# Row scaling moved behind a product, a shift carried as two extra columns, and part of the modulation rows summed by VectorE

## The chip, the core and the metric

The kernel runs on one core of a Trainium2 chip: TensorE (PE) for matrix products, VectorE (DVE), ScalarE (ACT), GpSimd (POOL), and SyncE (SP), which issues DMAs from memory. Each engine runs its own instructions in order and waits for others on semaphores. The metric is the device time of one execution in microseconds. Lower is better.

## The reference

Two transformer-like blocks run one after the other on 256 tokens of width 2048, in float32. What is computed:

```
# block 1
h = rms_norm(x, norm_gain);  proj = h @ w_in          # 2048 -> 8192: conv h,b,c,z and attention q,k,v,z
y_conv = rms_norm(b * conv(c * h_conv)) * silu(z_conv)
y_attn = rms_norm(causal_attention(norm(q), norm(k), v)) * silu(z_attn)   # 8 heads of 128
x = x + concat(y_conv, y_attn) @ w_out
# block 2, modulated by m = silu(c) @ w_ada + b_ada (6 blocks of 2048: sh_a sc_a g_a sh_m sc_m g_m)
h  = rms_norm(x, norm_attn_w) * (1 + sc_a) + sh_a
hc = rms_norm(ctx, norm_attn_w) * (1 + csc_a) + csh_a  # the same two blocks for c_ctx
q, k, v, u = split(h @ w_in_2);  kc, vc from hc @ w_in_2
x = x + g_a * (concat(window_attention, pool(u)) @ w_out_2)
hm = rms_norm(x, norm_mlp_w) * (1 + sc_m) + sh_m
x = x + g_m * (square(relu(hm @ w_up)) @ w_down)       # 2048 -> 8192 -> 2048
out = rms_norm(x, final_norm_w)
```

Only the blocks sh_a and sc_a are needed for c_ctx as well as for c. The other four are needed for c alone.

## The kernel before

**Tiles.** Activations lie transposed: feature on the 128 partitions, 256 tokens on the free axis (`T`), one tile for each of 16 groups of features (`KT`). Every product is written in units. A unit makes one 128x256 output tile from a 128x2048 strip of weights, which comes from memory as two halves of 512 KB into `raw`, a ring of four halves. ACT copies a half to `hi` (fp32r, L731), DVE makes `lo = raw - hi` (L1050), and PE adds up three products for each of the 16 tiles k: hi*x_hi, lo*x_hi, hi*x_lo (`half_unit`, L388; lines 400, 401 and 402). The activations `x` are kept as a pair too, 256 columns of high part and 256 of low part. The down product of the MLP does two of the three in one matmul of 512 columns (`pair_unit`, lines 426 and 427).

**Order.** Everything is written out by hand, and each engine has its own list. ACT and DVE call `split` in unit n for the halves that unit n+2 will use, as soon as PE has released the ring's slot (`w_used`). A unit's result leaves its bank by `evacuate` on ACT (L744) or by an addition on DVE, which counts `evac_done`; PE may start unit n+2 only then.

**Stages.** Units 0 to 31 are eight heads of four units (q, k, v, z): `head_body` on each engine; the scores, probabilities and values of a head are computed during the units of the next one. Units 32 to 63 are eight convolution tiles (`conv_body`). Units 64 to 79 are w_out of block 1 (`out_lap` on DVE, `out_body` on ACT, with the modulation of the context beside it, into `actC`). Then come 8 units of keys and values (80 to 87), 16 of queries and pooling, 16 of w_out_2 (`out_body` and the lap "dve w_out_2"), and four groups of 16 up and 16 down units. ACT and DVE run laps of a loop in most stages; in loops every address that depends on the lap costs register instructions on the engine.

**Modulation.** m needs 96 rows of `w_ada` of 1 MB each (6 blocks of 16 rows). PE takes one row in the middle of each of units 0 to 79, and the last block's during the following units: `ada_rows` (L432), four matmuls of 512 columns into the bank `ADA`, one for each column group, in plain float32 (two passes each). After 16 rows, ACT copies the bank (`ada_copy`, L752), PE turns it (`ada_turn`, L445), and DVE adds the bias (`ada_add`, L1120). The next block's first row waits for `ada_added`. SP loads the rows into two slots of `ada_raw`.

**The norm ahead of the MLP.** In each unit of w_out_2, DVE adds the result to `resid` (L1447), ACT squares it (L903), and DVE adds the square to `sqsum`. After the last one, PE sums over the partitions (`total_sums`), DVE, POOL and DVE make 1/rms on a diagonal, PE broadcasts it over the partitions into `BC`, and then DVE and ACT make the 16 tiles of `actA` four at a time (`norm_tiles`, L1094: times gain and `BC`, plus shift, high part, low part). Up unit 0 waits for each tile (`inA`).

```
def norm_tiles(first, n, gain, shift, src=resid):
    for k in range(first, first + n):
        ins = dve.scalar_tensor_tensor(t4[:, k % 4], src[:, k], gain(k), BC, ALU.mult, ALU.mult)
...
    for k in range(first, first + n):
        low(actA[:, k, 0:T], actA[:, k, T:2 * T], t4[:, k % 4], inA)
```

## Time and profile before

| | us |
|---|---|
| median of 3 runs | 1814.24 (1813.35 to 1815.23) |
| the profiled execution | 1812.95 |
| its span in the trace | 1811.3 |
| PE busy | 1671.5 (92%) |
| DVE busy | 1050.5 (58%) |
| ACT busy | 759.0 (42%) |
| modulation rows on PE (L441), 768 matmul passes | 102.2 busy |

The trace is that of one execution. Matmuls overlap, so "busy" of PE tells little of its pace; the distance from one start to the next does. PE's clock is granted by a throttle and is either full (2.4 GHz) or half (1.2 GHz). The page shows it in tenths over slices of 45 us.

### The profile page before, as it was taken

To read this page: it belongs to the slowest core of one execution; us is meant where nothing else is said; L and a number is where in the kernel's file an instruction comes from. 1 tells how busy PE (TensorE), PEld (TensorE's weight loads), DVE (VectorE), ACT (ScalarE), POOL (GpSimd) and SP (SyncE) were. 2 spreads that over 40 slices of the span, in tenths; PEclk is the share of its full clock that TensorE was granted. 3 is DMA by queue.
4 is the path that set the end of the run, shared out by engine and by line. 5 is a ranking of instruction groups with operands and counts; after the bars stand their busy time and mean duration, and the time that the engine had idled before them with its cause. 6 is when DMAs were issued, how large, how long until landed. Compare 5 with 4: busy or idle time off the path is not lost.

```text
span 1811.3 us, 34903 instructions
## 1 busy us (share of the span) xinstructions
PE 1671.5 (92%) x12462; PEld 1508.9 (83%) x12462; DVE 1050.5 (58%) x1568; ACT 759.0 (42%) x1068; POOL 31.5 (2%) x48
## 2 busy tenths in 40 slices
PE   3899999899988986999889869999999999999996
PEld 2788888788877876878779859989998999899985
DVE  4445454455556557467665575655556555555675
ACT  5344444334333334344344434434443454345442
POOL 0000000000000000000000000000000000000000
PEclk9899999899998998999999969999999999999998
DMA  7677777688874775673225515555555555555552
GB/s 311 242 268 251 276 269 258 214 302 288 301 283 167 286 258 192 256 291 117 94 70 175 176 68 185 185 186 181 180 186 192 183 183 186 185 184 183 185 189 92
DMA packets 88370, 374.71 MB, mean 207 GB/s; under 512 B 10256, under 2 KB 10768, under 8 KB 75488
## 3 DMA queue, kind: packets, MB, share of 16 engines
q1 hardware_dynamic: 87120, 369.54, 59.0%
q0 software_dynamic: 1168, 4.00, 0.7%
q8 instruction: 61, 1.00, 0.2%
q14 instruction: 21, 0.17, 0.0%
HBM read 371.40 MB, written 2.10 MB: 206 GB/s over the span
## 4 chain that ended last, share of the span: by engine, by line
issue 72%; PE 16%; DVE 8%; ACT 3%; POOL 0%; DVEq 0%; ACTq 0%; POOLq 0%
PE G L400 4%; PE G L401 4%; PE G L402 4%; DVE lo L1050 3%; ACT hi L731 1%; PE ADA L441 1%; PE M L624 1%; PE S L611 1%; PE ADA L638 1%; PE S L598 1%; DVE t L1097 0%; DVE resid L1512 0%; DVE sm L1344 0%; DVE blk L1050 0%; PE S L599 0%
## 5 line engine op out<-in xcount | busy, mean ns | idle before, releaser
L1050 DVE TENSOR_TENSOR lo<-raw,hi 128x1024 fp32r<-128x1024 f32 x496 | 607.8, 1225 | 427.9 <-ACT hi L731 396.1
L400 PE MATMUL G<-actA,hi 128*128 128x256 f32 x2368 | 691.8, 292 | 31.7 <-DVE actA L1050 31.1
L731 ACT ACTIVATE hi<-raw 128x1024 fp32r<-128x1024 f32 x496 | 525.6, 1060 | 387.3 <-PE G L427 194.6
L401 PE MATMUL G<-actA,lo 128*128 128x256 f32 x2368 | 676.5, 286 | 0.0
L402 PE MATMUL G<-actA,hi 128*128 128x256 f32 x2368 | 676.2, 286 | 0.0
L400 PEld LDWEIGHTS G<-actA,hi 128*128 128x128 f32 x2368 | 458.6, 194 | 93.0 <-issue 73.9
L401 PEld LDWEIGHTS G<-actA,lo 128*128 128x128 f32 x2368 | 459.2, 194 | 0.4
L402 PEld LDWEIGHTS G<-actA,hi 128*128 128x128 f32 x2368 | 458.7, 194 | 0.0
L426 PE MATMUL G<-actB,hi 128*128 128x512 f32 x1024 | 358.6, 395 | 0.0
L427 PE MATMUL G<-actB,lo 128*128 128x256 f32 x1024 | 287.5, 281 | 0.0
L426 PEld LDWEIGHTS G<-actB,hi 128*128 128x128 f32 x1024 | 192.2, 188 | 44.5
L427 PEld LDWEIGHTS G<-actB,lo 128*128 128x128 f32 x1024 | 194.1, 190 | 0.0
L400 PE MATMUL G<-actB,hi 128*128 128x256 f32 x496 | 144.4, 291 | 1.4 <-DVE lo L1050 0.8
L401 PE MATMUL G<-actB,lo 128*128 128x256 f32 x496 | 141.9, 286 | 0.0
L402 PE MATMUL G<-actB,hi 128*128 128x256 f32 x496 | 141.9, 286 | 0.0
L749 ACT ACTIVATE W<-G 128x256 f32<-128x256 f32 x80 | 30.7, 384 | 201.6 <-PE G L402 201.3
L400 PEld LDWEIGHTS G<-actB,hi 128*128 128x128 f32 x496 | 97.0, 195 | 15.4 <-issue 10.2
L441 PE MATMUL ADA<-ada_raw,cpad 128*32 128x512 f32 x768 | 102.2, 610 | 1.7 <-DMA ada_raw<-w_ada_dram 1.3
L401 PEld LDWEIGHTS G<-actB,lo 128*128 128x128 f32 x496 | 96.9, 195 | 0.1
L402 PEld LDWEIGHTS G<-actB,hi 128*128 128x128 f32 x496 | 96.7, 195 | 0.0
L749 ACT ACTIVATE t<-G 128x256 f32<-128x256 f32 x64 | 24.6, 384 | 118.5 <-PE G L402 118.5
L1050 DVE TENSOR_TENSOR acc<-acc,G 128x256 f32 x96 | 40.4, 421 | 34.3 <-PE G L427 31.7
(173 smaller groups left out, 1004.8 us busy)
## 6 DMA issues: line engine op xcount, KB each, us to landing
raw<-stream_dram SPq DMA_DIRECT2D x496, 512.0 KB, 4.2
ada_raw<-w_ada_dram SPq DMA_DIRECT2D x96, 1024.0 KB, 6.5
x_tok<-x_tok_dram SPq DMA_DIRECT2D x1, 2048.0 KB, 8.3
resid<-xT_dram SPq DMA_DIRECT2D x1, 2048.0 KB, 10.9
ctx_tok<-ctx_tok_dram SPq DMA_DIRECT2D x1, 2048.0 KB, 17.9
W<-ctxT_dram POOLq DMA_DIRECT2D x16, 128.0 KB, 6.1
out_dram<-resid SPq DMA_DIRECT2D x4, 512.0 KB, 2.6
ada_raw<-pool_w_dram POOLq DMA_DIRECT2D x1, 1024.0 KB, 6.9
```

What stands on the lines that cost most here:

```text
L400: pe.matmul(bank, hi[:, slot, cols], x[:, k, 0:T], start=(k == 0), stop=False, skip_group_check=True)
L401: pe.matmul(bank, lo[:, slot, cols], x[:, k, 0:T], start=False, stop=False, skip_group_check=True)
L402: m = pe.matmul(bank, hi[:, slot, cols], x[:, k, T:2 * T], start=False, stop=(k == KT - 1), skip_group_check=True)
L426: pe.matmul(bank[:], hi[:, slot, cols], x[:, k, :], start=(k == 0), stop=False, skip_group_check=True)
L427: m = pe.matmul(bank[:, 0:T], lo[:, slot, cols], x[:, k, 0:T], start=False, stop=(k == KT - 1), skip_group_check=True)
L441: m = pe.matmul(ADA[32 * g:32 * g + 32, :], cpad[:, 4 * (k % 4) + g, 6 - 2 * (k // 4):38 - 2 * (k // 4)], ada_raw[:, n % 2, g, :], start=( ...
L598: pe.matmul(bank[:, 0:T], q, kT[rows, s, :], start=True, stop=False, skip_group_check=True)
L611: m = pe.transpose(S[c][:, k * P:(k + 1) * P], probs[:, c, k * P:(k + 1) * P], ident[:])
L624: m = pe.matmul(M[64 * h:64 * h + 64, 0:T], v[:, k % 2, g:g + 64], turned[:, h, k, :], start=(k == 0), stop=(k == 3), tile_position=(0, 64 ...
L731: return act.activation(dst, src, ACT.Copy)
L749: act.activation(dst, G[j % 2][:, 0:T], func).then_inc(evac_done, 1)
L1050: return dve.tensor_tensor(dst, a, b, op)
```

## The change

There are two parts.

1. **The norm of the MLP.** The up product no longer takes the normed activations but `resid * scale_m`, which does not need 1/rms. It is made tile by tile inside w_out_2: ACT writes the high part with a scale from a pointer (L946 of the changed kernel), DVE the low part (L1525). The 1/rms of each token multiplies the result of a unit instead, on DVE, while the bank is emptied (`scaled`). The shift `sh_m` becomes two more columns of the activations (its high and its low part), so that 2 of the 3 matmuls of each step have 258 columns; the sum of the two result columns is a bias for each output feature, which ACT adds in the Relu. A tile of `actU` is 514 columns long, where one of `actA` is 512. `split` of a unit's second half now stands ahead of the Relu on ACT, and DVE waits for `relu_done`. The up units of group 0 start behind w_out_2 at once; sums and broadcast stand inside the first of them.
2. **Modulation.** Rows 32 to 63 (blocks g_a and sh_m) leave PE. DVE multiplies them by the condition into `part` (`part_take`, 4 instructions of 512 columns for a row, two rows for each head or convolution tile), and after four rows PE sums `part` over the partitions (`part_sums`, 4 matmuls of 1 column); DVE adds the bias (`part_add`). ACT issues the loads of these rows (`part_load`), into slot 1. PE keeps 64 rows: in units 0 to 63 one in every second unit (slot 0, SP), then as before. The loops over heads and convolution tiles on ACT and DVE are written out. Two turns of a block fall away; that at unit 80 moves behind unit 82, and `ada_copy` of block 1 moves ahead of the last tiles of the convolution's norm.

The diff, cut to its core:

```diff
-                unit(at, 1, actA, ada=4 * h + 1)
+                unit(at, 1, actA)
                 if prev:
                     head_turn()
-                unit(at, 2, actA, ada=4 * h + 2)
+                if prev and h % 2 == 0:
+                    part_sums(h // 2 - 1)
+                unit(at, 2, actA, ada=2 * h + 1)
...
+            def part_sums(n):
+
+                pe.wait_ge(ada_taken, 4 * (n + 1))
+                if n:
+                    pe.wait_ge(part_added, n)
+                for m in range(4):
+                    x = pe.matmul(PART[:, m:m + 1], part[:, m * P:(m + 1) * P], ones[:, 0:1], start=(m == 0), stop=(m == 3),
+                                  skip_group_check=True)
+                x.then_inc(part_summed, 1)
...
-            half_unit(at, 0, 0, actC, inC)
-            ada_turn()
-            half_unit(at, 0, 1, actC, inC)
+            unit(at, 0, actC, inC)
             total_sums(1)
...
             unit(at, 2, actC)
+            ada_turn()
             unit(at, 3, actC)
...
-            total_sums(2)
-            broadcast()
...
-                pair_units(8, base, actA, inA if g == 0 else None, 2 * KT)
+                if g == 0:
+                    at = At(base)
+                    pe.wait_ge(shift_ready, 1)
+                    half_unit(at, 0, 0, actU, inA, 2 * KT, extra=2)
+                    total_sums(2)
+                    half_unit(at, 0, 1, actU, inA, 2 * KT, extra=2)
+                    broadcast()
+                    up_unit(at, 1)
+                    up_units(7, base + 2)
+                else:
+                    up_units(8, base)
...
+            def part_load(n, row):
+
+                act.wait_ge(ada_taken, n)
+                src = t_in["w_ada"][row] if isinstance(row, int) else t_in["w_ada"][bass.ds(row, 1)].rearrange("a p n -> (a p) n")
+                act.dma_start(ada_raw[:, 1].rearrange("p k n -> p (k n)"), src).then_inc(ada_full[1], 16)
...
                 split(at, 0, 0)
+                if n:
+                    part_load(2 * n, 2 * KT + 2 * n)
...
                 split(at, 3, 0)
+                part_load(2 * n + 1, 2 * KT + 2 * n + 1)
...
+                    if not ctx_too:
+                        evacuated(at, j)
+                        act.activation(actU[:, u, 0:T], resid[:, u], ACT.Copy, scale=scale_m[:, u]).then_inc(x_hi, 1)
+                        own(x_hi)
                     square(at, j, (sq[:, j % 2:j % 2 + 1], resid[:, u]))
                     split(at, j)
...
+            def part_take(n):
+
+                if n % 4 == 0 and n:
+                    dve.wait_ge(part_summed, n // 4)
+                dve.wait_ge(ada_full[1], 16 * (n + 1))
+                k = n % 4 * 4
+                for m in range(4):
+                    w, c = ada_raw[:, 1, m, :], cpad[:, k + m, 6:7]
+                    if k + m == 0:
+                        seq(dve.tensor_scalar(part[:], w, c, None, ALU.mult))
+                    elif m < 3:
+                        seq(dve.scalar_tensor_tensor(part[:], w, c, part[:], ALU.mult, ALU.add))
+                    else:
+                        dve.scalar_tensor_tensor(part[:], w, c, part[:], ALU.mult, ALU.add).then_inc(ada_taken, 1)
+                        own(ada_taken)
...
                     split(at, j)
+                    dve.wait_ge(x_hi, turn.next("x_hi"))
+                    dve.scalar_tensor_tensor(actU[:, u, T + 2:], resid[:, u], scale_m[:, u], actU[:, u, 0:T], ALU.mult,
+                                             ALU.subtract).then_inc(inA, 1)
+                    own(inA)
                     add_squares(j % 2)
...
-            for b in range(4):
-                norm_tiles(4 * b, 4, lambda k: scale_m[:, k:k + 1], lambda k: adav[:, 0, SH_M + k:SH_M + k + 1])
...
-                        evacuated(at, j)
+                        summed(at, j)
+                        dve.reduce_sum(sm[:, 40 + j:41 + j], G[j % 2][:, T:T + 2], AX.X)
+                        tt(scaled[:, j], G[j % 2][:, 0:T], rstd_bc, ALU.mult).then_inc(evac_done, 1)
+                        split(at, j)
+                        dve.wait_ge(relu_done, turn.next("relu_done"))
                         seq(tt(t4[:, 2 + j], t4[:, j], t4[:, j], ALU.mult))
-                        split(at, j)
```

PE, head 1 before and head 2 after, between their units 1 and 2 (`S<-ident,W` turns the probabilities of the head before it). Before:

```order
L400 MATMUL G<-actA,hi 128x256
L401 MATMUL G<-actA,lo 128x256
L402 MATMUL G<-actA,hi 128x256
L481 MATMUL S<-ident,W 128x128 [waits probs_scaled]
L481 MATMUL S<-ident,W 128x128 x2
L400 MATMUL G<-actA,hi 128x256 [waits evac_done,lo_done]
```

After:

```order
L398 MATMUL G<-actA,hi 128x256
L488 MATMUL S<-ident,W 128x128 [waits probs_scaled]
L488 MATMUL S<-ident,W 128x128 x2
L456 MATMUL S<-ones,part 128x1 [waits ada_taken]
L456 MATMUL S<-ones,part 128x1 x3
L396 MATMUL G<-actA,hi 128x256 [waits evac_done,lo_done]
```

The sums of `part` stand here in every second head; the rows `ADA<-ada_raw,cpad` of units 1 and 3 are gone.

DVE in a head, from the scaling of the probabilities (`W<-W,sm`) to the sums of squares of q and k (`sm<-S`). Before:

```order
L1142 TENSOR_SCALAR W<-W,sm 128x256
L1050 TENSOR_TENSOR lo<-raw,hi 128x1024 [waits hi_done,probs_scaled]
L1050 TENSOR_TENSOR lo<-raw,hi 128x1024 [waits hi_done,lo_done] x2
L1091 COPY sm<-S 128x4 [waits sum_ready,lo_done]
L1050 TENSOR_TENSOR lo<-raw,hi 128x1024 [waits hi_done,sum_taken]
```

After:

```order
L1203 TENSOR_SCALAR W<-W,sm 128x256
L1088 TENSOR_TENSOR lo<-raw,hi 128x1024 [waits hi_done,probs_scaled]
L1088 TENSOR_TENSOR lo<-raw,hi 128x1024 [waits hi_done,lo_done]
L1088 TENSOR_TENSOR adav<-S,vec 128x4 [waits part_summed,lo_done]
L1178 TENSOR_SCALAR part<-ada_raw,cpad 128x512 [waits ada_full1,part_summed,part_added]
L1180 SCALAR_TENSOR_TENSOR part<-ada_raw,cpad,part 128x512 [waits dve_seq] x2
L1182 SCALAR_TENSOR_TENSOR part<-ada_raw,cpad,part 128x512 [waits dve_seq]
L1088 TENSOR_TENSOR lo<-raw,hi 128x1024 [waits hi_done,ada_taken]
L1129 COPY sm<-S 128x4 [waits sum_ready,lo_done]
```

A row of `w_ada` is taken between the splits of units 1 and 2, and another at the head's end.

DVE in one unit of w_out_2. Before:

```order
L1447 SCALAR_TENSOR_TENSOR resid<-G,adav,resid 128x256
L1055 REGISTER_ALU
L1050 TENSOR_TENSOR lo<-raw,hi 128x1024 [waits hi_done]
L1282 REGISTER_ALU [waits lo_done]
L1050 TENSOR_TENSOR sqsum<-sqsum,sq 128x256 [waits sq_ready]
L1039 REGISTER_ALU
L1055 REGISTER_ALU [waits sq_added]
L1050 TENSOR_TENSOR lo<-raw,hi 128x1024 [waits hi_done]
```

After:

```order
L1521 SCALAR_TENSOR_TENSOR resid<-G,adav,resid 128x256
L1093 REGISTER_ALU
L1088 TENSOR_TENSOR lo<-raw,hi 128x1024 [waits hi_done]
L1524 REGISTER_ALU [waits lo_done]
L1525 ISA [waits x_hi]
L1525 ISA
L1525 SCALAR_TENSOR_TENSOR actA<-resid,scale_m,actA 128x256
L1077 REGISTER_ALU
L1339 REGISTER_ALU [waits inA]
L1088 TENSOR_TENSOR sqsum<-sqsum,sq 128x256 [waits sq_ready]
L1077 REGISTER_ALU
L1093 REGISTER_ALU [waits sq_added]
```

The low part of the up product's input stands between the second split and the addition of the square, with four more instructions of its own on registers and waits.

## Rows read from the trace of the kernel before

**Rows 1.** Page, parts 1 and 2: busy times; PE clock in 40 slices.

```profile
PE 1671.5 (92%) x12462; PEld 1508.9 (83%) x12462; DVE 1050.5 (58%) x1568; ACT 759.0 (42%) x1068; POOL 31.5 (2%) x48
...
PEclk9899999899998998999999969999999999999998
```

**Rows 2.** Stretches: length, then busy time and instructions per engine, PEclk, DMA share, GB/s.

```profile
338.00:535.00 197.00, 196.63 (x1593) 169.37 (x1591) 108.01 (x144) 77.60 (x104) 0.00 (x0) 1.00 0.82 290
...
950.00:1033.00 83.00, 83.00 (x693) 82.89 (x691) 47.28 (x57) 36.57 (x44) 0.00 (x0) 1.00 0.55 180
1037.00:1072.00 35.00, 14.54 (x59) 12.91 (x60) 27.25 (x57) 9.52 (x21) 4.50 (x2) 0.51 0.09 31
```

**Rows 3.** PE in time, around a modulation row and a turn: start us, us, instruction.

```profile
130.45 0.28 PE L402 MATMUL G<-actA,hi 128*128 128x256 f32 x1
130.66 1.07 PE L441 MATMUL ADA<-ada_raw,cpad 128*32 128x512 f32 x8
...
131.88 0.28 PE L401 MATMUL G<-actA,lo 128*128 128x256 f32 x1
...
169.89 0.95 PE L449 MATMUL ADA<-sel,W 128*128 128x8 f32 x8
...
170.90 0.28 PE L401 MATMUL G<-actA,lo 128*128 128x256 f32 x1
```

**Rows 4.** A head: DVE's last scaling of probabilities, and PE's turn of them.

```profile
178.46 0.35 DVE L1142 TENSOR_SCALAR W<-W,sm 128x256 f32<-128x256 f32 x1
...
182.84 0.49 PE L481 MATMUL S<-ident,W 128*128 128x128 f32 x3
```

**Rows 5.** Loads of modulation rows, all 96.

```profile
DMA to landing us min/median/max: 4.8/6.5/11.6
```

**Rows 6.** Groups by line: form, count, busy us, mean ns, idle before.

```profile
L1344 DVE TENSOR_REDUCE sm<-S 128x1 f32<-128x512 f32 x32 | 19.9, 683 | 8.7 <-PE S L604 8.7
...
L1097 DVE SCALAR_TENSOR_TENSOR t<-resid,scale_m,M 128x256 f32<-128x256 f32 x16 | 7.7, 480 | 2.0 <-PE M L466 1.4
...
L766 ACT ACTIVATE W<-S,sm 128x256 f32<-128x256 f32 x8 | 4.4, 556 | 0.0
```

**Rows 7.** PE and DVE in time at the edges of stages (in brackets: idle before, releaser).

```profile
69.40 1.22 PE L466 MATMUL S<-W,ones 128*128 128x256 f32 x2 [6.85 <-DVE W L1077]
...
557.98 1.88 PE L449 MATMUL ADA<-sel,W 128*128 128x8 f32 x8 [7.61 <-ACT W L731]
...
684.88 1.88 PE L449 MATMUL ADA<-sel,W 128*128 128x8 f32 x8 [8.53 <-ACT W L731]
...
685.49 0.43 DVE L1050 TENSOR_TENSOR actC<-t,actC 128x256 f32 x1 [0.18 <-DVE lo L1050]
```

**Rows 8.** DVE in time, one unit of w_out_2.

```profile
983.66 0.48 DVE L1447 SCALAR_TENSOR_TENSOR resid<-G,adav,resid 128x256 f32 x1 [0.34 <-DVE lo L1050]
985.89 1.22 DVE L1050 TENSOR_TENSOR lo<-raw,hi 128x1024 fp32r<-128x1024 f32 x1 [1.75 <-ACT hi L731]
987.24 0.43 DVE L1050 TENSOR_TENSOR sqsum<-sqsum,sq 128x256 f32<-128x256 f32 x1
...
989.36 0.48 DVE L1447 SCALAR_TENSOR_TENSOR resid<-G,adav,resid 128x256 f32 x1 [0.34 <-DVE lo L1050]
```

**Rows 9.** From w_out_2 to the MLP: PE's sums and broadcast, ACT emptying up unit 1.

```profile
1040.30 1.01 PE L460 MATMUL S<-ones,sqsum 128*128 128x1 f32 x4 [7.20 <-DVE sqsum L1050]
...
1046.58 1.22 PE L466 MATMUL M<-W,ones 128*128 128x256 f32 x2 [5.27 <-DVE W L1077]
...
1077.38 0.38 ACT L749 ACTIVATE t<-G 128x256 f32<-128x256 f32 x1 [1.82 <-PE G L402]
```

**Rows 10.** PE in time, a down unit: 512 and 256 columns in turn.

```profile
1189.62 0.40 PE L426 MATMUL G<-actB,hi 128*128 128x512 f32 x1
1189.86 0.28 PE L427 MATMUL G<-actB,lo 128*128 128x256 f32 x1
1189.98 0.40 PE L426 MATMUL G<-actB,hi 128*128 128x512 f32 x1
```

More of the change, by code:

```diff
@@ L38 @@
 PAD = 8
+WIDE = 2 * T + 2
 VEC = {}
@@ L539, in _ @@
             for n in range(UNITS_OUT):
-                unit(At(U_OUT1), n, actB, inB, ada=U_OUT1 + n)
+                unit(At(U_OUT1), n, actB, inB, ada=2 * KT + n)
+                if n == 1:
+                    part_sums(7)
             def total_sums(n):
@@ L790, in head_out, with head_body @@
                 own(sq_ready)
-            def head_body(at, prev, block=None):
-                if block is not None:
-                    ada_copy(block)
+            def head_body(n, prev):
+                at = At(4 * n)
                 split(at, 0, 0)
+                if n:
+                    part_load(2 * n, 2 * KT + 2 * n)
                 if prev is not None:
@@ L1003, in _ @@
             pool_high(3)
-            with turn.lap(act, 4, "act w_out_2") as i:
-                out_body(At(U_OUT2, 4, i), i, False)
-            for k in range(KT):
-                high(actA[:, k, 0:T], t4[:, k % 4])
+            act.wait_ge(scale_ready, 3)
+            act.wait_ge(w_used, 2 * U_OUT2)
+            copy(actU[:, :, T:T + 1], adav[:, 0, SH_M:SH_M + KT].rearrange("p (k a) -> p k a", a=1)).then_inc(shift_hi, 1)
+            own(shift_hi)
+            for i in range(4):
+                out_body(At(U_OUT2 + 4 * i), i, False)
             for g in range(MLP_GROUPS):
@@ L1143, in head_scale, with head_body @@
                 own(probs_scaled)
-            def head_body(at, prev, h, block=None):
+            def head_body(n):
+                at, prev, h = At(4 * n), n > 0, slice(n, n + 1)
                 split(at, 0, 0)
-                if block is not None:
-                    ada_add(block)
                 if prev:
@@ L1155, in head_body @@
                 split(at, 1)
+                if prev and n % 2 == 0:
+                    part_add(n // 2 - 1)
+                part_take(2 * n)
                 split(at, 2, 0)
@@ L1178, in attn_tile, with conv_body @@
                 own(nt_ready)
-            def conv_body(at, tail, j, i, block=None):
+            def conv_body(j):
+                at, tail, i = At(4 * HEADS + 4 * j), j == 0, j - 1 if j else None
+                n = HEADS + j
                 split(at, 0, 0)
-                if block is not None:
-                    ada_add(block)
                 if tail:
+                    ada_add(0, 0)
                     head_max()
@@ L1198, in conv_body @@
                 split(at, 1)
+                if n % 2 == 0:
+                    part_add(n // 2 - 1)
+                part_take(2 * n)
                 split(at, 2, 0)
@@ L1247, in _ @@
             diagonal(0)
[L1248 to L1264 removed]
+            for n in range(1, HEADS):
+                head_body(n)
+            for n in range(CONV_TILES):
+                conv_body(n)
             attn_tile(7, slice(7, 8))
@@ L1284, in add_squares, with modulation_ready, out_lap @@
                 own(sq_added)
-            def out_lap(at, i, block=None):
+            def modulation_ready():
+                ada_add(1, 1)
+                for r in range(2):
+                    dve.scalar_tensor_tensor(scale_a[:, r], adav[:, r, SC_A:SC_A + KT], 1.0, col("norm_attn", 0, KT), ALU.add,
+                                             ALU.mult).then_inc(scale_ready, 1)
+                    own(scale_ready)
+            part_take(2 * KT - 1)
+            def out_lap(at, i, first=False):
                 for j in range(4):
@@ L1290, in out_lap @@
                     split(at, j, 0)
-                    if j == 0 and block is not None:
-                        ada_add(block)
+                    if j == 0 and first:
+                        modulation_ready()
+                    if j == 2 and first:
+                        part_add(7)
                     tt(resid[:, u], resid[:, u], summed(at, j), ALU.add).then_inc(evac_done, 1)
@@ L1439, in _ @@
             own(scale_ready)
+            dve.wait_ge(shift_hi, 1)
+            tt(actU[:, :, T + 1:T + 2], adav[:, 0, SH_M:SH_M + KT].rearrange("p (k a) -> p k a", a=1), actU[:, :, T:T + 1],
+               ALU.subtract).then_inc(shift_ready, 1)
+            own(shift_ready)
+            turn.base["inA"] = 2 * KT - turn.local.get("inA", 0)
             with turn.lap(dve, 4, "dve w_out_2") as i:
```

221 lines of the change are left out of this document (108 added, 113 removed).

## The prediction

> **What bounds the kernel now.** I read the page's busy times and clock slices first. PE is busy for 92% of the span, and its clock is full nearly everywhere [rows 1]. Then the stretches. In the convolution PE has no idle time while DVE works 108.0 and ACT 77.6 of 197.0 us, and the DMA engines are taken to 0.82 [rows 2]: there a matmul taken from PE is time won. Next, PE in time, for what one item costs from start to start [rows 3], and the edges of the stages, where PE stands idle behind ACT and DVE [rows 7]. Last, w_out_2, where PE's "83.00 of 83.00" misleads: DVE's additions to `resid` come every 989.36 − 983.66 = 5.70 us for a unit, and in between DVE waits 1.75 us for ACT's `hi` [rows 8]; a chain between DVE and ACT sets the pace there. Behind w_out_2 comes a stretch of 35 us with PE busy for 14.5, its clock at 0.51, the lower of the two levels [rows 2].
>
> **The change part by part.** The sum is made against the profiled execution, 1812.95 us, of which 1811.3 are the span; the median lies 1.3 above it.
>
> *Rows that leave PE.* From the matmul at 130.45 to the first one behind the row are 131.88 − 130.45 = 1.43 us [rows 3]. Two ordinary steps of 256 columns at 0.12 [rows 10] would be there anyway: a row costs 1.43 − 0.24 = 1.19 us. 32 rows leave stretches in which PE sets the pace: **−38.1**.
>
> *Turns and sums.* A turn costs 170.90 − 169.89 − 0.12 = 0.89 [rows 3]. Two fall away where PE is full: −1.8. `part_sums` are also four small float32 matmuls. Seven of them stand in full stretches, at the price of a turn: +6.2 (they have 1 column instead of 8; a lower end is half of it). The eighth lies in w_out, where PE idles. Together **+4.4**.
>
> *DVE and its queue.* One instruction of `part_take` is taken at 0.75 us: 480 ns for 256 columns of the same operation and 683 for a reduction over 512 columns [rows 6] bound it to about 0.68 to 0.96 (twice the 480). With 0.03 between them a row takes 3.1. 32 rows add some 100 us to DVE over 450 us of stage 1; at 108.0 of 197.0 [rows 2] DVE goes to about three quarters and stays under PE. Queued behind a row are the splits of unit 2, and PE waits for these. The slack: DVE ends the scaling of probabilities at 178.46 + 0.35 = 178.81 and PE turns them at 182.84 [rows 4], 4.0 later. Unit 1 on PE gets 1.2 shorter, and the row comes behind that scaling. So the 3.1 is covered, if thinly, by what remains. I allow **+0.5** for waits on a row's load. ACT, which issues it, waits there for `ada_taken` with its own splits queued behind. A load takes 4.8 to 11.6 us, median 6.5 [rows 5]; DVE first sees one from about 7.6, and PE would stand from about 9.9, by my count of the units between issue and use (1 us of slack on DVE, 2.3 more before PE).
>
> *The context's broadcast.* PE stood idle for 6.85 us ahead of 69.40, behind DVE's `W` [rows 7]. `part_take(1)` now stands ahead of that on DVE, and nothing covers it: **+3.1**.
>
> *The edges at 558 and 685.* Ahead of 557.98 PE waited 7.61 us for ACT's bank copy, then took 1.88 for the turn [rows 7]. `ada_copy` now stands earlier, but DVE has a row there and PE's first row waits for `ada_add`: **−1.2** (0 to −5). At 684.88 the turn waited 8.53 us [rows 7] in the middle of the first key unit. It is gone from there; the unit's half can end at about 686.6 instead of 691.9, a broadcast now stands behind half a unit, and later the first row of the last block waits about 0.4 for its bias: **−2.9**.
>
> *w_out_2.* ACT gets one more instruction per unit (556 ns for such a form), DVE one of 480 ns [rows 6] and four items on registers and waits, which I price like the 0.34 us that stand ahead of the addition now [rows 8]. Both engines are in the chain that sets the pace. Were both added in full it would be +1.4 a unit; were they to fit in DVE's wait of 1.75 [rows 8], 0. That wait is a wait for ACT, which has more to do as well, so I take the upper end: **+22.4** for 16 units, and +0.6 for the shift ahead of them.
>
> *Behind w_out_2.* From the sums at 1040.30 to the emptying of up unit 1 at 1077.38 are 37.1 us [rows 9]: sums, the norm's chain, a broadcast at 1046.58, 16 tiles of the norm made by DVE and ACT, and two units under the low clock. After: sums 1.0, half a unit at the low clock 5.1 (24 matmuls at 0.214), the broadcast 1.2 [rows 9], for which the chain of 5.27 [rows 9] is nearly covered (+0.3), and a full unit of 5.8, making 13.4. **−23.7**. The low clock's stretch shrinks from 35 us [rows 2] to about 10, since PE no longer idles for long.
>
> *258 columns.* A matmul of 512 starts its follower after 0.24 and one of 256 after 0.12 [rows 10], so 0.47 ns a column: two columns cost 0.94 ns in each of 2048 matmuls, **+1.9**, and 0 if the loading of the weights sets the pace. The rest of the MLP is unchanged: per unit DVE adds a reduction and waits for ACT's Relu, which I put at 5.0 to 5.7 us against PE's 48 × 0.12 = 5.76, so PE stays ahead by little.
>
> Sum: −38.1 + 4.4 + 0.5 + 3.1 − 1.2 − 2.9 + 22.4 + 0.6 − 23.7 + 1.9 = −33.0. Profiled 1780.0, median **1781**. Nearly all of it is part 2; part 1 alone comes to +1.2 by this sum, its gain at the edge being paid for in w_out_2.
>
> **The rivals.**
>
> (a) *The rows' loads come late.* Against it: with units 1.2 us shorter every second time, about 2.1 MB in 6.5 us make 320 GB/s, and 290 at a share of 0.82 [rows 2] give 353 at a full one. For it: that is over 0.9 full, and the longest load took 11.6 [rows 5], 1.7 beyond where PE stands. If that happened in each of 7 heads, the sum is +12: **1793**. The Trainium skill ("DMA: Bandwidth & Descriptors", Queues, rings and completion order) says that an engine serves the queues it has work for in turn, a packet each. By that, loads issued by ACT would no longer stand behind SP's weights but share with them, which shortens the row's landing and delays weights. No row here shows it, since all such loads were SP's.
>
> (b) *The low clock lasts.* The clock was low from 1037 to 1072 with PE nearly idle [rows 2]. If it stays low as long as it did, though PE works, 24 us more at the low level do 2.3 units at 10.3 instead of 5.8, +10.6: **1792**.
>
> (c) *w_out_2 hides what it gets*, because DVE's wait of 1.75 [rows 8] is the same time as ACT's: −22.4, **1759**.
>
> (d) *The other side: the tiles of 514 columns slow the matmuls of the up product.* The place is all 64 up units, 3072 matmuls, whose columns no longer begin where they did and are two more. The gain of 33 is used up at 33 / 3072 = 10.7 ns more for each (0.12 becomes 0.131), and from 12 ns on the kernel is slower by more than 0.2%. Against it: PE at 0.24 for 512 and 0.12 for 256 [rows 10] shows no fixed cost of a matmul that odd widths could bring out. For it: no tile of the kernel before has another stride or width than multiples of 256 columns, so its cost is not bounded from above by a row, other than by the pace at the low level (0.214, or +289 us); if it bites, it bites far: at +20 ns, **1841**. Beside this stands a rule of the Trainium skill ("Advanced Engine Details and Errata", Memory Cachelines): SBUF is read in lines of 16 bytes, at full pace while accesses hit the same line. By it 258 float32 columns touch 65 lines instead of 64, an estimated 1.6% of 120 ns on 3072 matmuls, +5.8 us in place of 1.9 and a time of 1785; it would not turn the sign.
>
> **How the numbers follow.** The forecast has 0.62, (a) 0.14, (b) 0.10, (c) 0.08, (d) 0.06. The forecast's own unknowns: w_out_2 (+22.4 may be 14), `part_take` (0.68 to 0.96 moves the context's gap by −0.3 to +0.8), `part_sums` (−3), the edges (−4 to +1), which make 1769 to 1786. To hold (a) and (b), and half of (c), the range is 1765 to 1795. A measurement of this kernel can tell about 0.2%, 3.6 us, from no change. Only (d) ends above; an overlap of (a) and (b) at their worst still lies at 1804. Faster 0.93, within 0.2% 0.01, slower 0.06.
>
> **What the profile after would show.** 64 rows of 8 passes on PE and 32 groups of one-column matmuls; PE without idle time in stage 1, DVE at three quarters there; `part_take` at about 0.75 us an instruction; a period of about 7.1 us in w_out_2 (5.7 would be (c)); no wait of 8 us for a turn near the start of the key units; a low clock of about 10 us behind w_out_2, not 34 (b); starts of 258-column matmuls 0.121 apart (0.131 or more would be (d)); waits of PE for `lo` in the heads behind a load that ACT issued would be (a). The prediction falls if w_out_2 keeps its pace, if DVE cannot carry the rows beside PE, or if the up units leave 5.8 us.

## The result and the profile after

The changed kernel takes **1774.24 us** (median of 4 runs, 1772.77 to 1778.43), the kernel before 1814.38 in the same comparison: a ratio of 0.978, interval 0.977 to 0.980, −40 us. The forecast was 1781 in a range of 1765 to 1795. The sum said −33.0 us, so 7 us came on top of it, and by parts it was further off than that.

The page after, parts 1 and 2, to be read beside [rows 1]:

```profile
PE 1635.3 (92%) x12254; PEld 1501.3 (85%) x12254; DVE 1165.5 (66%) x1798; ACT 768.3 (43%) x1067; POOL 32.0 (2%) x49
...
PEclk9899999899989999999999989999999999999998
```

PE has 36 us less to do, DVE 115 more. The clock slice at 6 tenths behind w_out_2 has gone.

Three stretches after (length, busy time and instructions of each engine, clock, DMA share, GB/s): the convolution, w_out_2, and the low clock behind it. They answer to [rows 2].

```profile
325.00:500.00 175.00, 175.00 (x1450) 161.35 (x1449) 141.90 (x191) 74.56 (x100) 0.00 (x0) 1.00 0.86 315
...
925.00:1008.00 83.00, 75.14 (x584) 70.89 (x584) 45.27 (x59) 36.58 (x48) 0.00 (x0) 1.00 0.47 151
...
1025.00:1035.00 10.00, 5.08 (x23) 5.08 (x24) 5.19 (x9) 3.04 (x4) 3.50 (x2) 0.51 0.35 105
```

In the convolution PE still has no idle time, with DVE at 141.90 / 175 = 81% and DMA at 0.86. In w_out_2 PE now stands idle for 8 of 83 us. The low clock lasts about 10 us.

From the first matmul of a stage to the first of the next, in us, in both traces, with the forecast's terms, and with what a mere shift of addresses does to the kernel before (the run before_pad, below):

| units | before | after | change | forecast | shift alone |
|---|---|---|---|---|---|
| 0 to 63, heads and convolution | 518.4 | 489.2 | −29.2 | −30.1 | −2.3 |
| 64 to 79, w_out | 128.0 | 129.9 | +1.9 | −1.2 | +0.5 |
| 80 to 87, keys and values | 78.6 | 74.5 | −4.2 | −2.9 | +0.3 |
| 88 to 103, queries, pooling | 173.7 | 175.5 | +1.8 | 0 | +3.2 |
| 104 to 118, w_out_2 but one | 101.6 | 115.6 | +14.1 | +23.0 (all 16) | +0.2 |
| 119, 120, the edge to the MLP | 44.0 | 25.5 | −18.5 | −23.7 | 0 |
| 121 to PE's last matmul, MLP | 728.1 | 723.9 | −4.2 | +1.9 | −7.7 |

With −0.4 ahead of unit 0 the changes make −38.8; the spans differ by 38.9.

DVE in one unit of w_out_2 after (start us, length us, instruction; idle time and its releaser in brackets), against [rows 8]:

```profile
961.35 0.48 DVE L1521 SCALAR_TENSOR_TENSOR resid<-G,adav,resid 128x256 f32 x1 [0.26 <-DVE lo L1088]
964.01 1.23 DVE L1088 TENSOR_TENSOR lo<-raw,hi 128x1024 fp32r<-128x1024 f32 x1 [2.18 <-ACT hi L755]
965.59 0.49 DVE L1525 SCALAR_TENSOR_TENSOR actA<-resid,scale_m,actA  x1 [0.35 <-DVE lo L1088]
966.20 0.43 DVE L1088 TENSOR_TENSOR sqsum<-sqsum,sq 128x256 f32<-128x256 f32 x1
966.75 1.23 DVE L1088 TENSOR_TENSOR lo<-raw,hi 128x1024 fp32r<-128x1024 f32 x1
968.23 0.48 DVE L1521 SCALAR_TENSOR_TENSOR resid<-G,adav,resid 128x256 f32 x1 [0.26 <-DVE lo L1088]
```

The unit takes 6.88 us here. DVE's wait for `hi` is 2.18 us (1.75 before), and the low part stands in line with 0.35 + 0.49.

How far DVE's addition to `resid` stands behind PE tells more than one unit. Before, PE's first matmul of units 105 and 119, and the addition that takes the result of the unit just ended (104 and 118):

```profile
946.55 0.28 PE L400 MATMUL G<-actB,hi 128*128 128x256 f32 x1
948.54 0.48 DVE L1447 SCALAR_TENSOR_TENSOR resid<-G,adav,resid 128x256 f32 x1 [0.39 <-DVE lo L1050]
...
1027.18 0.28 PE L400 MATMUL G<-actB,hi 128*128 128x256 f32 x1
1030.55 0.48 DVE L1447 SCALAR_TENSOR_TENSOR resid<-G,adav,resid 128x256 f32 x1 [0.34 <-PE G L402]
```

In these 14 units PE takes 80.63 us, 5.76 each, and DVE 82.01, 5.86 each: it falls from 1.99 to 3.37 us behind. After the change DVE takes 7.02 each over the same units, and from unit 108 on PE goes at that pace too.

DVE ahead of unit 32's modulation row; then PE in time: its new waits for a bias addition (units 32 and 64), the context's broadcast, and the sums behind w_out_2:

```profile
282.14 2.33 DVE L1180 SCALAR_TENSOR_TENSOR part<-ada_raw,cpad,part 128x512 f32<-128x512 f32 x3
284.50 0.75 DVE L1182 SCALAR_TENSOR_TENSOR part<-ada_raw,cpad,part 128x512 f32<-128x512 f32 x1
285.29 1.22 DVE L1088 TENSOR_TENSOR lo<-raw,hi 128x1024 fp32r<-128x1024 f32 x1
286.55 0.26 DVE L1088 TENSOR_TENSOR adav<-ADA,vec 128x16 f32<-128x16 f32 x2
```

```profile
286.86 1.06 PE L438 MATMUL ADA<-ada_raw,cpad 128*32 128x512 f32 x8 [2.83 <-DVE adav L1088]
...
532.98 1.94 PE L438 MATMUL ADA<-ada_raw,cpad 128*32 128x512 f32 x8 [3.63 <-DVE adav L1088]
...
69.63 1.22 PE L473 MATMUL S<-W,ones 128*128 128x256 f32 x2 [9.95 <-DVE W L1115]
...
1029.92 1.01 PE L467 MATMUL S<-ones,sqsum 128*128 128x1 f32 x4 [8.33 <-DVE sqsum L1088]
```

### The profile page after: what moved, and what is told of

It is laid out like the page before. It is cut to its first block, busy times and chain, and to the rows that moved or that the text cites. A ratio compares the mean times of both kernels' runs of the same rounds, so it can differ in the third digit from the quotient of the medians.

```text
span 1772.4 us, 33734 instructions
## 1 busy us (share of the span) xinstructions
PE 1635.3 (92%) x12254; PEld 1501.3 (85%) x12254; DVE 1165.5 (66%) x1798; ACT 768.3 (43%) x1067; POOL 32.0 (2%) x49
## 4 chain that ended last, share of the span: by engine, by line
issue 71%; DVE 12%; PE 11%; ACT 5%; DVEq 1%; POOL 0%; ACTq 0%; POOLq 0%
DVE lo L1088 5%; ACT hi L755 2%; PE G L396 2%; PE G L397 2%; PE G L398 2%; PE ADA L438 1%; PE M L636 1%; ACT sq L934 1%; DVE sqsum L1088 1%; DVE blk L1088 1%; PE S L610 1%; DVE sm L1413 1%; PE S L623 1%; PE ADA L650 1%; ACT actA L946 0%
## 5 line engine op out<-in xcount | busy, mean ns | idle before, releaser
L396 PE MATMUL G<-actA,hi 128*128 128x256 f32 (+1 forms) x2368 | 685.2, 289 | 20.1 <-DVE actA L1088 19.5
L397 PE MATMUL G<-actA,lo 128*128 128x256 f32 (+1 forms) x2368 | 672.5, 284 | 0.0
L398 PE MATMUL G<-actA,hi 128*128 128x256 f32 x2368 | 672.2, 284 | 0.0
L396 PEld LDWEIGHTS G<-actA,hi 128*128 128x128 f32 x2368 | 452.8, 191 | 54.5 <-issue 39.7
L397 PEld LDWEIGHTS G<-actA,lo 128*128 128x128 f32 x2368 | 452.4, 191 | 0.4
L398 PEld LDWEIGHTS G<-actA,hi 128*128 128x128 f32 x2368 | 451.6, 191 | 0.0
L438 PE MATMUL ADA<-ada_raw,cpad 128*32 128x512 f32 x512 | 69.1, 622 | 9.9 <-DVE adav L1088 6.7
L1180 DVE SCALAR_TENSOR_TENSOR part<-ada_raw,cpad,part 128x512 f32<-128x512 f32 x88 | 66.2, 752 | 7.2 <-DMA ada_raw<-w_ada_dram 4.2
## 6 DMA issues: line engine op xcount, KB each, us to landing
ctx_tok<-ctx_tok_dram SPq DMA_DIRECT2D x1, 2048.0 KB, 18.5
W<-ctxT_dram POOLq DMA_DIRECT2D x16, 128.0 KB, 5.5
```

Source lines behind the costliest of these rows:

```text
L396: pe.matmul(wide, hi[:, slot, cols], x[:, k, 0:T + extra], start=(k == 0), stop=False, skip_group_check=True)
L397: pe.matmul(wide, lo[:, slot, cols], x[:, k, 0:T + extra], start=False, stop=False, skip_group_check=True)
L398: m = pe.matmul(bank, hi[:, slot, cols], x[:, k, T + extra:2 * T + extra], start=False, stop=(k == KT - 1), skip_group_check=True)
L438: m = pe.matmul(ADA[32 * g:32 * g + 32, :], cpad[:, 4 * (k % 4) + g, 6 - 2 * (k // 4):38 - 2 * (k // 4)], ada_raw[:, slot, g, :], start=(k ...
L1180: seq(dve.scalar_tensor_tensor(part[:], w, c, part[:], ALU.mult, ALU.add))
```

## The experiments

All ratios are to the kernel before, run beside each.

### The two parts by themselves

part1 has only the changes of the norm, part2 only those of the modulation rows.

> The first part of the change alone (the norm behind the up product, two more columns), modulation as in the kernel before. The prediction's sum gives +1.2 us. Set against that are the two traces: from the start of w_out_2 to the first down unit the changed kernel is 4.6 us shorter, and the four groups of the MLP behind that 4.1 us, 3.4 of which lie in two down stages whose code did not change. Theory: both belong to this part, 1814.4 - 8.7 = 1805.7, with w_out_2 at about 6.9 us a unit and 512-column matmuls of the down product at 0.230 us in all four groups. Rival: the 3.4 us in the down stages come from elsewhere (part 2, or the placing of the program); then about 1809, with the first and third down stage at 0.236 for a 512-column matmul as before.

> The second part alone (32 modulation rows on DVE), the norm and the MLP as before. The prediction's sum gives -34.2 us, 1780.2. Theory from the two traces, unit by unit: stage 1 -29.6, w_out +1.9, keys and values -3.8, queries and pooling +1.4, together -30.1: 1784.3. PE waits 2.8 us in unit 32 and 3.6 in unit 64 for the bias addition of a block, which stands behind a row on DVE. Rival: parts 1 and 2 lean on each other (the ring's filling, DMA), then this is off by 3 us or more.

Measured: part1 **1806.3** (0.996, 0.994 to 0.997), part2 **1788.2** (0.986, 0.984 to 0.988). In part1 w_out_2 costs +14.3 us in 15 units, the edge gives 18.8 back, and the down stages are short, all as in the full change: the theory's 1805.7 held. Part 2's −26.2 is 8 short of the sum's −34.2 and 4 short of the theory's −30.1; its stage 1 lost 26.0 us, not 29.2. Part1 is shorter by 2.4 us in stage 1, though nothing was changed there; that unchanged code ran faster is what the group "Where the tiles lie" is about. The parts together give −34.3, the change −40.1. Of the 5.8 between them 0.9 are in stage 1 (−26.0 and −2.4 against −29.2) and 3.5 in the queries, where part1 shows +3.2, part2 +2.0 and the whole change +1.8. There the times go with the clock, as the paragraph on the low clock shows, and the parts don't add up.

### What set the pace of w_out_2

hi_first, on ACT:

```diff
                     if not ctx_too:
+                        split(at, j)
                         evacuated(at, j)
                         act.activation(actU[:, u, 0:T], resid[:, u], ACT.Copy, scale=scale_m[:, u]).then_inc(x_hi, 1)
                         own(x_hi)
                     square(at, j, (sq[:, j % 2:j % 2 + 1], resid[:, u]))
-                    split(at, j)
+                    if ctx_too:
+                        split(at, j)
```

> The changed kernel, with one order changed: in w_out_2 ACT makes the high part of the unit's second half of weights ahead of the high part of the activations and the square, not behind them. DVE does the same work. Theory: what slowed w_out_2 from 5.76 to about 6.95 us a unit is the loop resid (DVE), x_hi, square, hi (ACT), lo, x_lo, sqsum, lo (DVE); with hi taken out of it the unit is back at PE's 5.76: -13.8 us in w_out_2, and -5 to -6 at its end, since DVE no longer is 6 us behind PE and the sums wait less. 1774.2 - 19.5 = about 1755. Rival: DVE's or ACT's own list is the limit (they got 0.8 and 0.6 us a unit more): then w_out_2 stays at 6.5 us a unit or more, and the gain is under 6 us.

Measured: **1751.7** (0.966, 0.964 to 0.967), −22.5 against the changed kernel. Units 104 to 118 take 101.8 us (before the change 101.6), units 119 and 120 take 16.0 instead of 25.5. The whole is 3 us more than the theory's 19.5. PE waits 1.01 us for the last square instead of 8.33, and the clock doesn't fall there (1.00 from 995 to 1012 us):

```profile
995.00:1012.00 17.00, 13.71 (x111) 13.25 (x111) 10.95 (x16) 7.15 (x9) 4.50 (x2) 1.00 0.42 131
```

DVE in one unit of hi_first:

```profile
966.93 0.48 DVE L1523 SCALAR_TENSOR_TENSOR resid<-G,adav,resid 128x256 f32 x1 [0.71 <-PE G L398]
967.87 1.23 DVE L1090 TENSOR_TENSOR lo<-raw,hi 128x1024 fp32r<-128x1024 f32 x1 [0.46 <-ACT hi L755]
969.45 0.48 DVE L1527 SCALAR_TENSOR_TENSOR actA<-resid,scale_m,actA  x1 [0.35 <-DVE lo L1090]
970.06 0.43 DVE L1090 TENSOR_TENSOR sqsum<-sqsum,sq 128x256 f32<-128x256 f32 x1
970.75 1.23 DVE L1090 TENSOR_TENSOR lo<-raw,hi 128x1024 fp32r<-128x1024 f32 x1 [0.27 <-ACT hi L755]
972.76 0.48 DVE L1523 SCALAR_TENSOR_TENSOR resid<-G,adav,resid 128x256 f32 x1 [0.78 <-PE G L398]
```

The same instructions as in the changed kernel, and now DVE waits for PE ahead of `resid` (0.71, 0.78) instead of 2.18 for ACT. So neither engine had too much to do. What cost 14 us was the order: `hi` for the next weights stood on ACT behind two instructions that wait for `resid`, and so in a loop with DVE, whose addition to `resid` waits in turn behind the low part of those weights.

### The bias additions behind a row

ada_early: `ada_add(0, 0)` moves ahead of `part_take(15)`, and `modulation_ready`, which starts with the addition of block 1, ahead of `part_take(31)`:

```diff
+                if n == HEADS - 1:
+                    ada_add(0, 0)
                 part_take(2 * n + 1)
...
                 if tail:
-                    ada_add(0, 0)
                     head_max()
...
+            modulation_ready()
             part_take(2 * KT - 1)
...
-                    if j == 0 and first:
-                        modulation_ready()
```

> The changed kernel, with the bias addition of blocks 0 and 1 on DVE ahead of the row (rows 15 and 31 of DVE's 32) that stands before it, not behind it. Theory: PE's waits of 2.83 us at 286.86 and 3.63 at 532.98 for this addition go, and with them some us at the low clock: -6.5 to -9, 1766 to 1768. Rival: another wait takes their place (the row on DVE is then later, and with it the splits that PE needs next): -3 or less, 1771 or more.

Measured: **1771.8** (0.977, 0.975 to 0.978), −2.5: the rival's outcome, but only at one of the two places. Units 32 to 35 went from 44.3 to 39.8 us: −4.6, more than the wait of 2.83, and the mean clock of this stretch rose from 0.88 (287 to 320 us) to 0.96 (282 to 315). At unit 64 another wait came in, for the row that SP may load only after DVE's last one; units 64 and 65 stayed at 28.0:

```profile
536.06 1.07 PE L438 MATMUL ADA<-ada_raw,cpad 128*32 128x512 f32 x8 [2.67 <-DMA ada_raw<-w_ada_dram]
```

Units 0 to 3 and 36 to 63 took 3.4 us more, though the order of instructions differs only at their end, and hid most of the first gain. Why they did is not shown.

### How much cover DVE had

take_six, two more multiplications a row:

```diff
                         seq(dve.scalar_tensor_tensor(part[:], w, c, part[:], ALU.mult, ALU.add))
+                        if m:
+                            seq(dve.scalar_tensor_tensor(part[:], w, c, part[:], ALU.mult, ALU.add))
```

> The changed kernel, where DVE multiplies two of the four column groups of each modulation row twice (6 instructions of 512 columns at 0.752 us instead of 4; the gate and the shift come out other than the reference's by this). It doubles half of the cost that the prediction called covered, if thinly: +1.5 us on DVE for each of 32 rows, 48 us. In the convolution DVE goes from 81% to about 93% of its time, in the heads from 70% to 80%. Theory: still covered in the heads and nearly in the convolution; what shows are the places where DVE is waited for already (the context's broadcast, the unit behind row 15 and row 31, the last part sum), four of them at 1.5: +6 to +12, 1780 to 1786. Rival: the cover was used up by the 3.1 us: each further 1.5 us is paid nearly in full, +30 to +48, 1804 or more.

Measured: **1794.1** (0.989, 0.987 to 0.990), +19.9 against the changed kernel: between the two. 20 of the 48 us on DVE were paid, 16.2 of them in units 4 to 63, not at the edges alone: the three convolution tiles of units 36 to 47 take 1.0 us more each. In the convolution DVE is busy for 156.04 of 180 us (87%), PE for 171.97:

```profile
325.00:505.00 180.00, 171.97 (x1379) 158.25 (x1380) 156.04 (x214) 68.69 (x91) 1.01 (x1) 0.96 0.79 293
```

"Covered, if thinly" was right for 3.1 us and would have been wrong for 4.6.

### The two columns

cols272 and cols320 take more columns, cols256 gives the extra ones to the first wide matmul of a unit only:

```diff
-                bank, wide = G[j % 2][:, 0:T], G[j % 2][:, 0:T + extra]
+                bank = G[j % 2][:, 0:T]
...
-                    pe.matmul(wide, hi[:, slot, cols], x[:, k, 0:T + extra], start=(k == 0), stop=False, skip_group_check=True)
-                    pe.matmul(wide, lo[:, slot, cols], x[:, k, 0:T + extra], start=False, stop=False, skip_group_check=True)
+                    pe.matmul(G[j % 2][:, 0:T + (extra if k == 0 else 0)], hi[:, slot, cols], x[:, k, 0:T + (extra if k == 0 else 0)], start=(k == 0), stop=False, skip_group_check=True)
+                    pe.matmul(bank, lo[:, slot, cols], x[:, k, 0:T], start=False, stop=False, skip_group_check=True)
```

> The changed kernel, with the two wide matmuls of each step of the up product taken over 272 columns instead of 258 (the 14 more read on into the low part, and their results are used by nobody). In the traces the up units pace at 0.1198 us a matmul both with 256 and with 258 columns, while a pair of 512 and 256 columns of the down product takes 0.230 + 0.115, that is 0.45 ns a column. Theory: there is a floor of about 0.120 us a matmul in the up product that is not the columns, and the two extra columns hide under it; 272 columns at 0.45 ns are 0.1224, just above: +2.5 ns on 2048 matmuls, +5 us, 1779. Rival: each column adds 0.45 ns on top, and the two columns' 1.9 us were hidden by something else: +6.3 ns, +13 us, 1787.

> As the run before, with 320 columns. Floor: 320 x 0.45 = 0.144 us in place of 0.120, +24 ns on 2048 matmuls, +50 us, 1824. Each column adds: 62 x 0.45 = +28 ns, +57 us, 1831. The two are told apart by the distance from one start of a 320-column matmul to the next: 0.144 or 0.148.

> The changed kernel, with the two more columns multiplied in the first of the 32 wide matmuls of a unit only, and 256 columns in the others (the shift reaches the product through the first tile's high part alone, so most of it is left out). Same tiles of 514 columns, same addresses. In the changed kernel the three matmuls of a step of the up product take 0.3596 us together, in the kernel before 0.3600, at 272 columns 0.3716. Theory: a floor of 0.360 for such a step hides the two columns: still 0.359 to 0.360, 1774. Rival: the 514-column tiles or the addresses made the steps shorter, and the two columns took that back at 0.44 ns a column: 0.3578, -1.8 us, 1772.4.

Measured: cols272 **1785.8** (0.985, 0.984 to 0.987), cols320 **1840.5** (one run), cols256 **1772.5** (0.977, 0.975 to 0.978). In all three the theory of a floor was wrong and the rival right or nearer: 320-column matmuls are followed after 0.148 us and not 0.144. PE in time, the first matmul of the second group's up stage and of its down stage, in cols272 and cols320:

```profile
1213.82 0.29 PE L396 MATMUL G<-actA,hi 128*128 128x272 f32 x1
...
1308.96 0.40 PE L422 MATMUL G<-actB,hi 128*128 128x512 f32 x1
```

```profile
1231.02 0.31 PE L396 MATMUL G<-actA,hi 128*128 128x320 f32 x1
...
1337.05 0.39 PE L422 MATMUL G<-actB,hi 128*128 128x512 f32 x1
```

So an up stage takes 95.14 and 106.03 us. The changed kernel has 92.06 and cols256 91.44 (512 wide matmuls each). The step from 256 to 258 columns costs 0.62 us, 1.2 ns a matmul; that from 258 to 272 costs 6.0 ns, 0.43 ns a column; that from 272 to 320 costs 21.3 ns, 0.44 a column. Nothing is hidden: the columns are paid from the first on. They didn't show because the whole stage had become shorter, and cols256, at the same addresses, shows by how much: 91.44 against 92.16 before. (Another 7 us of cols320 come from its down stages, which take 90.45 instead of 88.75, four times; the next group comes to this.)

### Where the tiles lie

In the convolution, matmuls of 256 columns follow each other after 0.1198 us before, 0.1188 in part1 and 0.1186 after the change, in code that is the same for them. What part1 and the changed kernel share is that `actA` got 128 bytes longer on each partition, so that `actB`, `raw`, `hi` and `lo` begin 128 bytes further on. before_pad is the kernel before with this alone:

```diff
-        actA = sb("actA", [P, KT, 2 * T], F32R)
+        actA_all = sb("actA", [P, KT * (2 * T + 2)], F32R)
+        actA = actA_all[:, 0:KT * 2 * T].rearrange("p (k n) -> p k n", k=KT)
```

before_pad_1k has `KT * 2 * T + 256` there, 1024 bytes. before_unrolled leaves the tiles alone and writes out two up units on PE.

> The kernel before, word for word, but for 128 bytes a partition of unused room behind the tile actA, as the changed kernel has there, so that actB, raw, hi and lo begin 128 bytes later. Theory: this placing alone is why matmuls of 256 columns in the convolution follow each other after 0.1186 us in the changed kernel and in part 1 alone, and after 0.1197 before, and why 512-column ones of the first and third down stage take 0.230 and not 0.236: then this run shows 0.1186 and 0.230, -2.2 us in stage 1 and -3.4 in the down stages, about 1808.5 in all. Rival: placing does nothing, the code or the stride of the up product does it: 1814, 0.1197 and 0.236.

> The kernel before, with the first two up units of the first group written out on PE ahead of a loop of seven laps, as the changed kernel has them, and no other difference. Theory that the placing of data sets the pace of the down stages: unchanged, 0.236 us for a 512-column matmul in the first and third, 0.230 in the others, 1814. Rival, that the placing of PE's code sets it: 0.230 in all four, or in the other two, up to -3.4 us.

> The kernel before with 1024 unused bytes a partition behind the tile actA, in place of the 128 that brought it from 1814.0 to 1807.4 us. In the kernel before all large tiles (resid, actA, actB, raw, hi, lo) follow each other at multiples of 16 KB. Theory: the low bits of the addresses matter, how the weights and activations lie to each other within 1 KB; a shift by a whole KB changes none of them: 1814, 0.1197 us a matmul in the convolution, 0.120 in the up units and 0.236 for 512 columns in the first down stage. Rival: any shift off the 16 KB grid does it: 1807.5, 0.1188, 0.1187 and 0.230.

Measured: before_pad **1807.4** (0.997, 0.995 to 0.998), before_pad_1k **1814.5** (1.000, 0.999 to 1.001), before_unrolled 1814.0 (one run). PE at three edges, the start of the first down stage, of the second up stage and of the second down stage: before, before_pad, before_pad_1k, and after the change.

```profile
1157.83 0.40 PE L426 MATMUL G<-actB,hi 128*128 128x512 f32 x1
...
1248.28 0.28 PE L400 MATMUL G<-actA,hi 128*128 128x256 f32 x1
...
1340.44 0.40 PE L426 MATMUL G<-actB,hi 128*128 128x512 f32 x1
```

```profile
1158.47 0.39 PE L427 MATMUL G<-actB,hi 128*128 128x512 f32 x1
...
1247.22 0.28 PE L401 MATMUL G<-actA,hi 128*128 128x256 f32 x1
...
1338.35 0.40 PE L427 MATMUL G<-actB,hi 128*128 128x512 f32 x1
```

```profile
1157.99 0.40 PE L427 MATMUL G<-actB,hi 128*128 128x512 f32 x1
...
1248.45 0.28 PE L401 MATMUL G<-actA,hi 128*128 128x256 f32 x1
...
1340.61 0.40 PE L427 MATMUL G<-actB,hi 128*128 128x512 f32 x1
```

```profile
1123.09 0.40 PE L422 MATMUL G<-actB,hi 128*128 128x512 f32 x1
...
1211.85 0.28 PE L396 MATMUL G<-actA,hi 128*128 128x258 f32 x1
...
1303.91 0.39 PE L422 MATMUL G<-actB,hi 128*128 128x512 f32 x1
```

| | down stage | up stage |
|---|---|---|
| before | 90.45 | 92.16 |
| before_pad (128 bytes) | 88.75 | 91.13 |
| before_pad_1k (1024 bytes) | 90.46 | 92.16 |
| after | 88.76 | 92.06 |

128 bytes give 1.7 us in that down stage and 1.0 in each up stage; 1024 bytes give nothing. So what matters is how the tiles lie within 1 KB. Writing out two units in PE's code changed nothing (one run). In the traces of the kernel before, part2, before_pad_1k and before_unrolled a down stage is at 88.8 or at 90.5, with no fixed pattern (before_pad_1k has the first, second and fourth slow, before the first and third); with the 128 bytes it was at 88.8 in all but one kernel, cols320, which had it slow in all four. What picks the pace within one layout stays open. So does what collides: other offsets, and which of the four shifted tiles does it, weren't tried.

### All three orders mended

best is hi_first and ada_early together, and `part_take(1)` moves behind the context's norm. The expectation names the addition of block 0 alone, but the kernel has both additions early. What it has beyond the two edits shown above:

```diff
             mean_square(ss[:, 2:4], D)
             diagonal(0)
+            part_take(1)
...
-                part_take(2 * n + 1)
+                if n:
+                    part_take(2 * n + 1)
```

> The changed kernel with three orders changed: in w_out_2 ACT's high part of the second half ahead of the high part of the activations and the square (1751.7 by itself); the bias addition of block 0 ahead of DVE's row 15 (-4.6 in units 32 to 35 by itself); DVE's row 1 behind the context's norm, not ahead of it (the gap at 59 us is 10.3 now, 7.2 before the change: -3.1). Theory: they add up: 1751.7 - 7.7 = 1744. Rival: what is gained ahead of a stage is given back at the next edge, as in the run with both additions early (-4.6 in units 32 to 35, but -2.5 in all): 1748 to 1750.

Measured: **1744.2** (0.961, 0.960 to 0.963), the sum's 1744. Units 0 to 3 take 40.7 us (43.8 after the change), units 32 to 35 39.8 (44.3), and w_out_2 with the edge 117.5 (141.1). Not all of it adds up: units 64 to 87 take 2.6 us more than after the change (in unit 65 PE waits 3.75 for a row's load, as in ada_early), and the queries 2.2 less. This beats both kernels: 30 us under the changed one.

## Why the prediction was right, and where it wasn't

**The rows off PE** (−38.1). Unit 37, which lost its row, went from 6.94 to 5.70 us: 1.24, of which 1.19 are the sum's and 0.05 come from the placing. (The matmul at 131.88 is the second behind the row, not the first; the sum takes off two steps, so 1.19 is right.) One `part_take` instruction takes 0.752 us, where the sum had 0.75 between bounds of 0.68 and 0.96:

```profile
L1180 DVE SCALAR_TENSOR_TENSOR part<-ada_raw,cpad,part 128x512 f32<-128x512 f32 x88 | 66.2, 752 | 7.2 <-DMA ada_raw<-w_ada_dram 4.2
```

`part_sums` cost 0.89 in unit 17 (6.92 against 6.03 in unit 13), the price of a turn. The context's broadcast waited 9.95 us, 3.1 more, as in the sum. The cover held too: in units 4 to 31 and 36 to 62 PE never waits longer than 0.2 us. This part of the working held line by line.

**What it missed in stage 1.** The text followed the queue behind `part_take(1)` but not behind `part_take(15)`. There DVE's addition for block 0 ended 9.6 us into unit 32 instead of 6.8, PE waited these 2.8, the clock fell, and it cost 4.6 in all (ada_early, best). It was made up for in good part by the placing (−2.3), by the allowance of 0.5 that nothing used, and by units 4 to 31, which came out 1.2 shorter than their rows, sums and turn make against before_pad; so −30.1 against −29.2 is right partly by luck. The same step at the next edge, "−1.2 (0 to −5)", had the row on DVE in view and not its size. PE waited 3.63 for the addition where it had waited 7.61 for the turn, but ahead of that 1.60 and 1.79 for tiles of the norm (`actB`), which before had become ready during that wait. Two waits for loads, 2.43 and 0.80, stand later in the stage (the longest before was 0.58), and w_out came out at +1.9.

**w_out_2** (+22.4 and −23.7). The failed step is the first reading, "a chain between DVE and ACT sets the pace there". PE set its own: its units took 5.76 us in the trace of before, 48 matmuls at 0.120. The 5.70 between two additions to `resid` was the shortest of a pattern of four (5.88, 5.79, 5.71, 6.10), which comes to 5.86 over the 14 units shown above. So the chain was there, and even 0.1 us slower than PE, but PE ran ahead of it on what the ring had ready. What the additions do to the chain the sum had nearly right, 7.02 instead of 7.1. What it had wrong is who pays. PE kept its 5.76 through unit 107, until DVE was over 6 us behind, and only then went at the chain's pace: +14.1 for 15 units where the sum had 23.0 for 16. What seemed saved came back in part at the edge. DVE ended 6 us behind PE, and PE did half an up unit and then waited 8.33 for the last square. The sum put nothing there: it let the half unit vanish in the 7.20 that PE had waited before. The edge gave 18.5 and not 23.7. Together that is −4.5 against −0.7, two errors of 8.9 and 5.2 that point opposite ways. The rival "w_out_2 hides what it gets" was wrong as well, but hi_first shows that it could have hidden all of it, with one line of ACT's list moved.

**The low clock** lasted 10 us behind w_out_2, as said, and rival (b) fell. But low stretches came in elsewhere: in the queries the mean clock was 0.98 over 174 us before and 0.96 over 175 after, which is 7 and 14 us at the low level, beside the same gaps of PE (2.3, 6.2 and 2.2 us, in all three kernels below). Stretches of the queries before, in before_pad and after, with the clock as the column before the last two:

```profile
752.00:926.00 174.00, 162.75 (x1304) 140.74 (x1303) 120.27 (x224) 76.36 (x139) 0.53 (x1) 0.98 0.48 173
```

```profile
750.00:927.00 177.00, 165.40 (x1302) 142.61 (x1301) 120.05 (x223) 76.45 (x138) 0.54 (x1) 0.95 0.48 170
```

```profile
720.00:895.00 175.00, 163.41 (x1297) 140.66 (x1296) 119.53 (x220) 76.44 (x138) 0.53 (x1) 0.96 0.48 172
```

The stage's +1.8 (and +3.2 in before_pad, which has 17 us at the low level) goes with that. Why the clock fell at a gap in one run and not in another is not shown.

**The MLP** (+1.9). Measured −4.2, made of −7.7 by the placing and +3.5 by the change (against before_pad, whose up stages take 91.13). Of the 0.93 us in an up stage, 0.62 are the two columns (cols256). 0.31 are left; the tiles of 514 columns are the likeliest cause, but no run has them alone. The sum had 0.94 ns a wide matmul and nothing for the tiles, so this term was right in kind and about half of what was measured. The rule on memory lines of the Trainium skill ("Advanced Engine Details and Errata", Memory Cachelines) made +5.8 of it; the traces show 3.5, between the two. Rival (d) would have needed 33.

**Keys and values** (−2.9). Unit 80, where the turn was, went from 17.9 to 13.8 us: the wait of 8.53 for the turn is gone, and one of 5.54 for the context's tiles (`actC`) stands there now. The stage gave −4.2, 1.3 more than the sum.

**Loads** (rival (a)) were no trouble in the heads. Rows that ACT issues land after a median of 6.4 us, those of SP after 6.7 (6.5 before), and the halves of weights after 3.5 (4.2 before), with the DMA engines at 0.86 in the convolution.

The total was nearer than its terms. Errors of −6.1 (MLP), −3.8 (w_out_2 and edge), −1.3 (keys and values) and −0.4 (start) stood against +0.9 (stage 1), +3.1 (w_out) and +1.8 (queries). So the total is near by luck as well: errors of 11.6 us one way and 5.8 the other. The largest was one that no row of before could have priced: the placing of tiles, 6.6 us in before_pad.

## What to carry to other kernels

When an instruction goes into an engine's list, look for what stands behind it that someone waits for; here three such instructions (a weight split, a bias addition, a norm's diagonal) cost 30 us, and moving each past its neighbour gave them back. Before saying that a chain sets the pace, compare its mean period over many units, not between one pair, with PE's own count times its step. Here they were 5.86 and 5.76: the chain had no slack left, and what was added to it was paid late, once PE's lead was spent. And when stages that weren't changed change their pace, suspect that buffers have moved, and test it with a pad and nothing else.

## What was not expected of the hardware

A shift of four large tiles by 128 bytes a partition took the step of a 256-column float32 matmul from 0.1198 to 0.1188 us in the convolution and from 0.1200 to 0.1187 in the up loops, and that of a 512-column one from 0.236 to 0.230 in the first down stage: 6.6 us in 1814. In w_out_2 the step stayed at 0.1200. A shift by 1024 bytes did nothing.
